# Expert phase of a two-layer backbone: gathers issued further ahead, transposes between the first products, second product in plain fp32 straight from the loaded weights

## What is computed

```python
def moe(xt, router_w, router_bias, w1, w3, w2, ...):     # D_MODEL 1024, 64 experts, top 8, EXPERT_HIDDEN 256
    ...                                                   # idx, wts: 8 experts and weights of each token
    padded = (counts + EBLK - 1) // EBLK * EBLK           # EBLK = 128: each expert's tokens in blocks of 128
    ...
    def expert_block(args):
        tok, e = args
        xb = xpad[tok]
        h = jax.nn.silu(xb @ w1[e]) * (xb @ w3[e])
        return h @ w2[e]
    ...
    routed = zeros.at[slot_tok].add(yb * slot_w[:, None])
```

## Time and profile before

| what | value |
|---|---|
| median of 3 runs | 3825.52 us (3824.91 to 3831.3) |
| profiled execution | 3826.97 us, span of its core 3825.2 us |
| PE busy | 3093.2 us, 81% of the span |
| DVE busy | 2148.1 us, 56% |
| ACT busy | 1586.6 us, 41% |
| POOL busy | 504.5 us, 13% |
| HBM traffic | 596.95 MB read, 92.37 MB written |
| expert phase of layer 0 | from 1063.65 us (first weight load) to 2108.7 us (first read by `combine`) |
| expert phase of layer 1 | from 2811.96 us to 3800.6 us |

### The profile page before, as it was taken

One profiled execution on the slowest core, in us unless ns is written; L12 is line 12 of the kernel. 1 busy time (PEld: TensorE's weight loads), 2 busy tenths in 40 slices (PEclk: granted clock), 3 DMA queues, 4 the chain that ended last, 5 costly groups with the idle time before them and its releaser, 6 DMA issues. The chain is left out here.

```text
span 3825.2 us, 56362 instructions
## 1 busy us (share of the span) xinstructions
PE 3093.2 (81%) x12323; PEld 2137.6 (56%) x12324; DVE 2148.1 (56%) x3840; ACT 1586.6 (41%) x2332; POOL 504.5 (13%) x609
## 2 busy tenths in 40 slices
PE   5698999996768887888887499787668888878884
PEld 0245677754356666666665244554346666666763
DVE  0334333333477777666676520784367776777575
ACT  0133222221156556555554311342136665665564
POOL 0000000000012222222222000000012222222221
PEclk8695555586879999899998699899678888888997
DMA  9601000003079979888788410100358998999786
GB/s 403 262 0 47 1 1 1 1 1 120 33 283 300 293 247 304 268 269 275 252 252 241 159 55 0 47 1 1 120 192 276 307 307 287 299 301 302 230 292 191
DMA packets 138176, 690.47 MB, mean 181 GB/s; under 512 B 15464, under 2 KB 23272, under 8 KB 81000
## 3 DMA queue, kind: packets, MB, share of 16 engines
q1 hardware_dynamic: 93312, 526.56, 36.4%
q0 software_dynamic: 43776, 159.40, 17.9%
q10 hardware_dynamic: 1000, 3.41, 0.2%
HBM read 596.95 MB, written 92.37 MB: 180 GB/s over the span
## 5 line engine op out<-in xcount | busy, mean ns | idle before, releaser
L1630 DVE TENSOR_TENSOR e_w13l<-ring,e_w13h x512 | 593.2, 1221 | 71.1 <-issue 45.7
L1538 ACT CAST e_w13h<-ring x512 | 498.2, 1044 | 153.7 <-issue 92.8
L1456 PE MATMUL e_psH<-e_w13h,e_xh 128*128 x1184 | 468.6, 396 | 7.9 <-ACT e_xh L1558 7.9
L1456 PE MATMUL e_psH<-e_w13l,e_xh 128*128 x1184 | 465.6, 393 | 0.0
L1441 PE MATMUL e_psT<-m_id,e_xg 128*128 128x128 f32 x1200 | 211.6, 332 | 247.6 <-DMA e_xg<-h_rows,e_gidx 247.4
L1480 PE MATMUL e_psY<-e_w2h,e_gh 128*128 128x512 f32 x592 | 318.9, 539 | 90.8 <-DVE e_w2l L1617 80.8
L455 PE MATMUL psP<-ring,ho 128*128 128x512 f32 x800 | 349.5, 592 | 0.0
L1395 POOL DMA_INDIRECT y_rows<-e_y,e_sidx x148 | 290.3, 1962 | 375.4 <-ACT e_y L1566 219.4
L1441 PEld LDWEIGHTS e_psT<-m_id,e_xg 128*128 128x128 f32 x1200 | 176.1, 203 | 266.9 <-issue 252.7
L1617 DVE TENSOR_TENSOR e_w2l<-ring,e_w2h 128x1024 fp32r<-128x1024 f32 x256 | 301.5, 1219 | 27.6 <-ACT e_w2h L1527 20.2
L1558 ACT CAST e_xh<-e_psT 128x512 fp32r<-128x512 f32 x300 | 166.7, 588 | 305.3 <-PE e_psT L1441 303.2
(11 more groups left out here) (265 smaller groups left out, 4278.3 us busy)
## 6 DMA issues: line engine op xcount, KB each, us to landing
ring<-in_exp_w SPq DMA_DIRECT2D x388, 1024.0 KB
ring<-in_ada_w SPq DMA_DIRECT2D x48, 1024.0 KB, 13.3
ring<-in_c_w_in SPq DMA_DIRECT2D x6, 2048.0 KB
bc<-mod_rows SPq DMA_DIRECT2D x4, 1536.0 KB, 8.1
r_bc<-mod_rows SPq DMA_DIRECT2D x4, 1536.0 KB
ring<-in_sh_w SPq DMA_DIRECT2D x6, 1024.0 KB
h_rows<-r_hrow SPq DMA_DIRECT2D x10, 512.0 KB, 2.6
y_rows<-r_y SPq DMA_DIRECT2D x10, 512.0 KB, 2.6
```

The lines of the kernel that those rows point to most:

```text
L1456: nc.tensor.matmul(psH[par][:], xh[par][:, k * P:(k + 1) * P], w[:, bass.DynSlice(half, 1), :, k, :], start=(k == 0 and i == 0), stop=False)
L1538: nc.scalar.copy(w13h[:, bass.DynSlice(half, 1), :, k, :].rearrange("p o u k n -> p (o u) (k n)"), raw13[:, bass.DynSlice(half, 1), :, k, ...
L1630: nc.vector.tensor_tensor(low, raw, high.bitcast(F32), ALU.subtract).then_inc(w13_lo, 1)
```

## The change

Gathers are issued four blocks ahead in place of two, and are freed from the scatter's landing: indices and weights of all blocks are kept in `idxs` and `gws` (a column for each block), and POOL copies a column before each gather and each scatter. Spare slots now have an index beyond the last row, and the gather skips indices above T, so that only used slots (and one spare row) are fetched. The table's spare rows move from the front of `h_rows` and `y_rows` to their end. PE transposes the rows of block b+1 between the first products of block b, one transpose behind each pair. `index(b+4)` and `turn_gate(b)` are put between the products of `down(b-1)`, which now runs after `hidden(b)`. ACT computes SiLU in one instruction, and DVE's first multiplication goes. The second product is 4 matmuls in plain fp32, from `gt` (one copy of the transposed gate) and from w2 as it was loaded: `split2`, `rest2` and the two halves of gate and w2 are gone. In place of `w2_lo`, `load2` waits for the new semaphore `w2_used`, which ACT raises behind `rows_out` of an expert's last block.

```diff
@@ load2 on SP
                 wait_for(sp, w2_in, 16 * o)
                 sp.sem_inc(sp_clear, 1)
-                wait_for(sp, w2_lo, 2 * (o - 1))
+                wait_for(sp, w2_used, o - 1)
@@ gather and scatter on POOL
+                wait_for(pool, xt_mm, 2 * (b - 1))
+                pool.wait_ge(idx_ready, b + 1)
+                nc.gpsimd.tensor_copy(gidx[par][:], idxs[:, at_block(b)]).then_inc(g_copied, 1)
+                pool.wait_ge(g_copied, b + 1)
+                nc.gpsimd.indirect_dma_start(xg[par][:], None, s.hrows[l], bass.IndirectOffsetOnAxis(ap=gidx[par][:, 0:1], axis=0),
+                                             bounds_check=T, oob_is_err=False).then_inc(gathered[par], 16)
...
+                nc.gpsimd.tensor_copy(sidx[par][:], idxs[:, at_block(b)]).then_inc(s_copied, 1)
+                pool.wait_ge(y_ready, b + 1)
-            def keep(b, par):
...
@@ down on PE
-                for k in range(KF):
-                    pe.wait_ge(w2_lo, 2 * o + k + 1)
-                    for c in range(2):
-                        for i, w in enumerate((w2h, w2l)):
-                            nc.tensor.matmul(psY[...], gh[par][:, k * P:(k + 1) * P], w[:, k, c * 512:(c + 1) * 512], ...)
-                pe.wait_ge(g_lo, b + 1)
+                pe.wait_ge(w2_in, 16 * o + 16)
                 for k in range(KF):
                     for c in range(2):
-                        mm = nc.tensor.matmul(psY[...], gl[par][:, k * P:(k + 1) * P], w2h[:, k, c * 512:(c + 1) * 512], ...)
+                        mm = nc.tensor.matmul(psY[...], gt[par][:, k * P:(k + 1) * P],
+                                              raw2[:, bass.DynSlice(half, 1), k, c * 512:(c + 1) * 512], start=(k == 0), stop=(k == KF - 1))
+                        if k == 0 and c == 1:
+                            first()
+                        if k == 1 and c == 0:
+                            second()
@@ PE, one step
+                hidden(b, par, code, lambda k: turn(b + 1, m, 1 - par, k))
+                down(b - 1, 1 - par, before, lambda: index(b + 4, par, e), lambda: turn_gate(b))
@@ ACT
-                nc.scalar.activation(ge[:], psH[par][:, 0:F], ACT.Sigmoid).then_inc(e_ready, 1)
+                nc.scalar.activation(ge[:], psH[par][:, 0:F], ACT.Silu).then_inc(e_ready, 1)
...
+                nc.scalar.activation(ysb[par][:], psY[:], ACT.Copy, scale=gws[:, at_block(b)]).then_inc(y_ready, 1)
+                code = code_of(act, b + 1)
+                with act.If((code & 7) == 0):
+                    act.sem_inc(w2_used, 1)
...
             def step(b, par):
-                expo(b, par)
-                gate(b - 1, 1 - par)
-                rows_in(b + 1, 1 - par)
-                split13(b + 2, range(PIECE))
-                rows_out(b - 1, 1 - par)
-                split2(b)
+                rows_in(b + 1, 1 - par)
+                silu(b, par)
+                split13(b + 2, range(2))
+                gate(b, par)
+                if not isinstance(b, int) or b > 0:
+                    rows_out(b - 1, 1 - par)
+                split13(b + 2, range(2, PIECE))
@@ DVE
             def step(b, par):
-                gate(b - 1, 1 - par)
-                indices(b + 2, par)
-                rows_in(b + 1, 1 - par)
-                silu(b, par)
-                choose(b + 3, 1 - par)
-                rest13(b + 2, range(PIECE))
-                rest2(b)
+                rows_in(b + 1, 1 - par)
+                product(b, par)
+                indices(b + 3)
+                choose(b + 5, 1 - par)
+                rest13(b + 2, range(2))
+                rest13(b + 2, range(2, PIECE))
```

More of the change, by code:

```diff
@@ L1470, in turn_gate, with down @@
                 tr.then_inc(gt_mm, 1)
[L1472 to L1474 removed]
+            def down(b, par, code, first, second):
+                o, half = order_in(code), half_in(code)
+                pe.wait_ge(gt_ready, b + 1)
                 wait_for(pe, y_ready, b)
[L1476 to L1482 removed]
+                pe.wait_ge(w2_in, 16 * o + 16)
@@ L1515, in _, with step @@
-            down(2 * n, 0)
+                        mm = nc.tensor.matmul(psY[:, c * 512:(c + 1) * 512], gt[par][:, k * P:(k + 1) * P],
+                                              raw2[:, bass.DynSlice(half, 1), k, c * 512:(c + 1) * 512], start=(k == 0), stop=(k == KF - 1))
[3 more added lines that the diff above has]
+                            second()
+                mm.then_inc(y_mm, 1)
+            def step(b, m, par, first=False):
+                code, e = code_of(pe, b), expert_of(pe, b + 4)
+                before = None if first else code_of(pe, b - 1)
+                hidden(b, par, code, lambda k: turn(b + 1, m, 1 - par, k))
+                if first:
+                    index(b + 4, par, e)
+                    turn_gate(b)
+                else:
+                    down(b - 1, 1 - par, before, lambda: index(b + 4, par, e), lambda: turn_gate(b))
@@ new lines, in _ @@
+            n = pairs(pe)
+            for b in range(4):
+                index(b, b % 2, expert_of(pe, b))
+            for k in range(KD):
+                turn(0, 0, 0, k)
+            step(0, 0, 0, True)
+            step(1, 1, 1)
+            with pe.Fori(0, n - 1) as i:
+                step(2 * i + 2, i + 1, 0)
+                step(2 * i + 3, i + 2, 1)
+            m = ending(pe)
+            code, before = code_of(pe, m + 2), code_of(pe, m + 1)
+            hidden(m + 2, 0, code, lambda k: None)
@@ L1517, in _ @@
+            down(m + 1, 1, before, lambda: None, lambda: turn_gate(m + 2))
+            down(m + 2, 0, code, lambda: None, lambda: None)
         @block.scalar
         def _(act):
-            def split2(b):
-                code = code_of(act, b)
-                with act.If((code & 7) == 0):
-                    o, half = order_in(code), half_in(code)
-                    act.wait_ge(w2_in, 16 * o + 16)
-                    wait_for(act, y_mm, b)
-                    for k in range(KF):
-                        nc.scalar.copy(w2h[:, k:k + 1, :], raw2[:, bass.DynSlice(half, 1), k, :]).then_inc(w2_hi, 1)
@@ L1581, in _ @@
             step(1, 1)
-            step(2, 0)
             with act.Fori(0, n - 1) as i:
+                step(2 * i + 2, 0)
                 step(2 * i + 3, 1)
-                step(2 * i + 4, 0)
             m = ending(act)
+            silu(m + 2, 0)
             gate(m + 2, 0)
+            rows_out(m + 1, 1)
             rows_out(m + 2, 0)
@@ L1671, in _ @@
             step(1, 1)
-            step(2, 0)
             with dve.Fori(0, n - 1) as i:
+                step(2 * i + 2, 0)
                 step(2 * i + 3, 1)
-                step(2 * i + 4, 0)
-            gate(2 * n, 0)
+            m = ending(dve)
+            product(m + 2, 0)
 def combine(nc, s, a, l, tiles):
```

193 lines of the change are left out of this document (72 added, 121 removed).

## The result

The changed kernel takes 3903.35 us (median of 4 runs, 3898.79 to 3906.61) against 3825.22 for the kernel before beside it: a ratio of 1.0205, 95% interval [1.0182, 1.0227]. It is 2.0% slower, well clear of the noise; 3933 was predicted.

What follows compares the result with a forecast made beforehand. Wait loop through w2 and w13 loads binds one-block experts: 78 x 17.0 + 10 x 7 + 58 x 11.0 = 2034 us against 1927, 107 more, giving 3933 us, 2.8% slower; range 3770 to 4040.

Steps and rivals of the forecast that it cites:

- The chain over one block: In one-block experts, rows_out(b) releases load2(b+2), then load13(b+4), two split pieces, gate, rows_out(b+1): 17.0 us each.
- ACT idle on the ring: ACT's w13 split would wait for the ring's DMA some 5 us in each bound step.
- The number of long steps: Steps bound by the loop of loads, counted along ACT's timeline: 78 of 146, in 10 runs.
- Term 1: e_y and the hop to SP's issue of the w2 load: 1.3 us, or 0.8 if signalled early; 1.2 taken.
- Term 2: From load2's issue to ACT's w13 split, with scatter in the window: bounds 10.7 and 14.3 us; 13.2 taken.
- The rival with the full scatter price: Loads give way to the whole scatter: 18.1 us per block in bound steps, 4019 us; chance 0.20.
- Term 3: ACT's two w13 split pieces, gate's copy and two handovers: 2.6 us, 2.4 to 3.0.
- The turn: One round of the loop, from one e_y's start to the next: 17.0 us, from 13.9 to 18.6.
- a sign of being wrong: Prediction wrong if bound steps are under 15.6 us, or if ACT's w13 split does not wait for the ring.
- The free steps: Steps not bound by loads cost PE's own work: 58 at 11.0 us.
- The ends of a run: Behind each of 10 runs of bound steps, one step takes only about 7 us.
- The clock: PE's granted clock would be lower in the long steps, with PE busy about 10.8 of 17 us.

Runs made afterwards that it cites:

- old_second: Changed kernel with the earlier second product back (w2 and gate halves, 12 fp32r products, load2 waiting for DVE's w2 split): 3727.52 us, 0.9732 of the kernel before.
- late_signal: Changed kernel with ACT's sequencer waiting until e_y is written before it raises w2_used: 4097.91 us, 1.0701 of the kernel before.
- full_gather: Changed kernel with bounds_check dropped from the gather, so all 128 slots are fetched: 3901.8 us, 1.0193 of the kernel before.
- reads_apart: Changed kernel with PE's three table reads spread to where its engine has queued work: 3852.11 us, 1.0052 of the kernel before.
- ahead_reads: Changed kernel with w1/w3 loads issued ahead of w2 loads and PE's three table reads spread: 3515.26 us, 0.9191 of the kernel before.
- old_second_index: Changed kernel with the earlier second product, spread table reads, and PE's index products behind the gate's transposes: 3607.18 us, 0.9431 of the kernel before.
- old_second_reads: Changed kernel with the earlier second product back and PE's three table reads spread: 3791.15 us, 0.9904 of the kernel before.

## Why the prediction was right, and where it was off

**The mechanism: right, and shown.** The chain over one block was called from the order of SP's waits, and three runs agree: breaking it gives 210 us, a later signal adds 195, and without the new wait (`old_second`) the time is under that of before. Also right: ACT idle on the ring in each long step (8.4 us, where I said 5), and PE waiting for gathered rows for 4.7 us in the whole run. The number of long steps held as well: 78 in 10 runs by counting, and in the trace 76 of 14 us and more in 10 runs from one `e_y` to the next (73 from one `e_ge` to the next).

**Term 1, e_y and the signal: 1.2 predicted, -0.8 measured.** I put it down as 1.3, or 0.8 if ACT's sequencer doesn't wait for the end. The load left 0.79 us *before* `e_y` began, though the signal stands behind `e_y` in the program, and while the engine was still at the split, two instructions ahead. So the sequencer doesn't wait even for the start of `e_y` before it goes on to the branch and the signal. With a wait for the end of `e_y` (`late_signal`) the load goes 1.47 us after its start. The Trainium skill, "Advanced Engine Details and Errata", section "Sequencer and Instruction Queues", says that the sequencer pushes an engine instruction into a queue, where it waits, and itself starts to execute a control instruction. The trace agrees, with 0.79 us here.

**Term 2, the transfers: 13.2 predicted, 13.4 measured, but not by its parts.** I had built it as loads 11.3, half a gather gone 0.6, and 2.5 of a scatter's 3.6. The gather is free in this place (`full_gather`), and the scatter costs about 1.3. So by difference the two loads behind each other take nearer 12 than 11.3, an estimate. The total held, and parts that were wrong offset each other: that is luck. The rival with the full scatter price gave a turn of 18.1, and the long steps average 14.9. The rule that the prediction set beside it (the Trainium skill, "DMA: Bandwidth & Descriptors", section "Queues, rings and completion order": a DMA engine goes round its queues by whole packets) is neither borne out nor refuted by that: no run shows whose packets went first.

**Term 3, two pieces and the gate: 2.6 predicted, 2.2 measured.** The three copies overlap at their ends: 1.99, 0.36 and the start of `e_y` in 2.16 us.

The turn is -0.8 + 13.4 + 2.2 = 14.8 us, where 17.0 was said, and 2.0 of the 2.2 us between them are term 1. That is under the 15.6 that I had named both as the turn that breaks even and as a sign of being wrong, so by that sign the prediction failed, though its number did not. With 14.9 in place of 17.0 and all else as I had it, my sum is 78 x 14.9 + 70 + 638 = 1870 us, 57 less than before: a faster kernel. It is slower all the same because of what I put too low elsewhere:

**The free steps: 11.0 predicted, 12.4 measured.** I summed PE's products, and `reads_apart` and `ahead_reads` show that sum to be right (11.2 and 10.9). What I left out is its sequencer. Before, one read stood at the head of each of `index`, `hidden` and `down`; now all three stand ahead of `hidden` with nothing queued, and expose 1.1 to 1.4 us in each step. I looked at the matmuls that move, not at the reads that the order puts together. Spreading them gives back 51 of the 78 us that the change loses: `reads_apart` is only 0.5% slower than the kernel before.

**The ends of a run: 7 predicted behind it, 9.8 to 12.0 measured, and nothing ahead of it, where 2.5 to 4.3 are.** From one `e_y` to the next, as the prediction counts, the step behind a run takes 9.8 to 12.0 us. And the first step of each of the 10 runs takes 17.4 to 19.2 us, where the 66 others average 14.9: some 30 us in all that I had no term for. From one `e_ge` to the next these ends show as most of the 15 steps between 13 and 14 us.

With the measured sizes the sum is 76 x 15.3 + 70 x 11.8 = 1992 us from first to last `e_y`, beside the 2034 that I added up. The long steps took 1163 us in place of 1326, 163 less; the others 829 in place of 708, 121 more. So 3933 came near because two errors offset each other, and with the first alone even the direction would have been wrong: in both there is luck. The layers show it: layer 0 lost 28 us, where I had 6, and layer 1 lost 38, where I had 101.

**The clock: right in kind.** In a long step PE stands still for 2.87 us in front of the index, and then the granted clock falls. PE's row, then stretches of 1 us:

```profile
3456.06 0.55 PE L1430 MATMUL e_psI<-tab,e_sel 128*128 x4 [2.87 <-DVE e_idxs L1598]
```

```profile
3457.00:3458.00 1.00, 1.00 (x5) 0.62 (x4) 0.42 (x1) 0.00 (x0) 1.00 (x1) 0.97 1.06 324
3458.00:3459.00 1.00, 1.00 (x2) 0.00 (x0) 0.00 (x0) 0.00 (x0) 0.35 (x1) 0.50 1.00 287
...
3463.00:3464.00 1.00, 1.00 (x4) 0.77 (x3) 0.90 (x1) 1.00 (x3) 0.00 (x0) 0.50 0.00 0
3464.00:3465.00 1.00, 1.00 (x5) 0.66 (x5) 1.00 (x2) 1.00 (x3) 0.00 (x0) 0.62 0.98 147
```

From 3458 to 3464 us PE runs at the lower of its two levels, 1.2 GHz. It costs the chain nothing here: the next `e_y` (3463.97) follows ACT's split and the gate's copy at once, and the next split stands idle for the ring's DMA again, for 7.27 us up to 3476.77. The next long step, 3463.97 to 3478.93, has a mean of 0.97, so it isn't every one. Over all 73 long steps the mean is 0.92 (in 44 of them it is under 0.95), over the others 0.99.

## What to carry to other kernels

When a buffer's release moves from the engine that copies out of it to the one that consumes the result, look at what else is queued behind the load that waits for it, and count over how many blocks the loop of waits then closes. A cheaper operation that shortens such a loop of waits to fewer blocks can lose more than it saves; here the order of two loads was worth 210 us, more than the whole change had cost. And judge an operation with its surroundings mended on both sides: the fp32 product costs 176 us in one load order and gains 88 in the other. Ask of every term of a sum what the result would be with that term alone put right: here the direction hung on one.

Reads from memory into a sequencer's registers belong behind work that is already queued, one at a time. And an edit that lets PE come earlier to a product can be lost again if the input of that product isn't moved with it.

## What the runs showed of the hardware

- ACT's sequencer raised a semaphore 0.8 us before the instruction ahead of it in the program began on the engine, and while the split, two instructions ahead, still ran (measured at the load that the signal lets go). A wait for that instruction's own semaphore moved the load to 1.5 us after its start.
- A table read on PE's sequencer takes 0.30 us, and with its register operations 0.75 us to the next. Three in a row showed as 1.43 us of PE idle, put down to an engine that had long been done.
- Gathers with and without the unused slots cost the same in a chain of loads (3901.8 and 3903.35 us); the same skipping on the scatter with its add gave 45 us.
- PE idle for 2.1 us, at a granted clock of 1.00, was followed by 3.4 us at 0.50 to 0.51. With the index moved (`old_second_index`) the clock between 2880 and 3500 us was 0.97 in place of 0.89; in `old_second`, where PE's longest wait for `e_idxs` in layer 1 was 1.5 us, it was 1.00. How much of the 184 us between `old_second_reads` and `old_second_index` is the clock, and how much the wait itself, no run here separates.
